# Twelve gate tiles of a two-layer encoder kernel in pairs: seven block products for eight, with the sums of frames on VectorE

## The reference, cut to what matters

```
proj = jnp.einsum('btd,de->bte', x, w_in)          # 512 + 2048 columns
cq = rms_norm(proj[..., :Q_LORA], q_norm_g)        # 4 tiles of 128: query latent
gate = proj[..., Q_LORA:]                          # 16 tiles of 128: one a head
kv = jnp.einsum('btd,de->bte', x, w_dkv)           # key/value latent, 256 + 64
...
out = jnp.einsum('bte,ed->btd', o * jax.nn.silu(gate), w_out_b)
```

## Time and profile before

| | |
|---|---|
| median of 3 runs | 1863.83 us (1863.42 to 1863.83) |
| profiled execution | 1863.33 us, its span 1861.5 us |
| granted TensorE clock, mean | 0.998 |
| VectorE, ScalarE, GpSimd busy | 56%, 40%, 23% of the span |
| HBM | 95 GB/s over the span |

### The profile page before, as it was taken

The page is one execution under the profiler, slowest core; times in us unless marked ns, Lnnn a source line. Parts: engine busy times, 40 slices in busy tenths (PEclk is TensorE's granted clock), DMA queues, the critical chain, the costliest instruction groups (busy, mean ns, idle before and its releaser), DMA issues.

```text
span 1861.5 us, 30229 instructions
## 1 busy us (share of the span) xinstructions
PE 1849.0 (99%) x11250; PEld 1734.6 (93%) x11250; DVE 1046.2 (56%) x1852; ACT 741.8 (40%) x1307; POOL 429.6 (23%) x341
## 2 busy tenths in 40 slices
PE   9999999999999999999999999999999999999998
PEld 8899999999988999999999999999999999998886
DVE  3126565556768512432466676666766679853642
ACT  4234324333422221221355565555555567651100
POOL 0013133223311010000042432434324344400000
PEclk9999999999999999999999999999999999999999
DMA  8120222222255312233302111111121185553521
GB/s 264 57 87 33 76 83 84 72 83 73 70 195 164 131 46 73 83 100 120 100 27 67 42 55 55 56 51 46 51 75 38 30 255 185 189 203 127 166 86 45
DMA packets 162059, 178.91 MB, mean 96 GB/s; under 512 B 23376, under 2 KB 137424, under 8 KB 161712
## 3 DMA queue, kind: packets, MB, share of 16 engines
q1 hardware_dynamic: 155632, 158.08, 26.8%
q10 hardware_dynamic: 6160, 19.14, 2.9%
q0 software_dynamic: 176, 0.43, 0.1%
HBM read 130.86 MB, written 46.76 MB: 95 GB/s over the span
## 4 chain that ended last, share of the span: by engine, by line
PE 94%; DVE 2%; ACT 2%; issue 1%; DMA 1%; POOL 0%; DVEq 0%; ACTq 0%; SPq 0%; POOLq 0%
PE ps L124 27%; PE ps L126 26%; PE ps L125 26%; PE ps L2126 3%; PE ps L2105 2%; PE ps L2104 2%; PE ps L550 1%; PE ps L510 1%; PE ps L576 1%; PE ps L559 1%; PE ps L579 1%; ACT h_p L2239 1%; PE ps L539 1%; PE ps L561 1%; PE ps L2682 1%
## 5 line engine op out<-in xcount | busy, mean ns | idle before, releaser
L2016 POOL TENSOR_SCALAR h_p<-h_p,h_rsum 128x128 f32<-128x128 f32 (+3 forms) x127 | 217.8, 1717 | 420.5 <-DVE h_rsum L2368 420.1
L124 PE MATMUL ps<-act_h,a_w_l 128*128 128x384 f32 x576 | 202.0, 351 | 0.0
L126 PE MATMUL ps<-act_h,a_w_h 128*128 128x384 f32 x576 | 192.9, 335 | 0.0
L125 PE MATMUL ps<-act_l,a_w_h 128*128 128x384 f32 x576 | 192.8, 335 | 0.0
L124 PE MATMUL ps<-act_h,m_c_l 128*128 128x384 f32 x480 | 160.9, 335 | 0.0
L126 PE MATMUL ps<-act_h,m_c_h 128*128 128x384 f32 x480 | 160.4, 334 | 0.0
L125 PE MATMUL ps<-act_l,m_c_h 128*128 128x384 f32 x480 | 160.4, 334 | 0.0
L118 DVE TENSOR_TENSOR h_pt_l<-ps,h_pt_h 128x128 fp32r<-128x128 f32 (+2 forms) x192 | 100.5, 552 | 60.2 <-ACT h_pt_h L113 59.8
L113 ACT ACTIVATE h_pt_h<-ps 128x128 fp32r<-128x128 f32 (+2 forms) x192 | 86.8, 489 | 88.3 <-PE ps L2126 88.1
L2239 ACT ACTIVATE h_p<-ps,h_mx 128x128 f32<-128x128 f32 (+7 forms) x128 | 94.8, 741 | 67.1 <-DVE h_mx L2364 66.7
L124 PE MATMUL ps<-o_w,o_g 128*128 128x512 f32 x288 | 112.3, 390 | 0.0
(11 more groups left out here) (326 smaller groups left out, 4955.0 us busy)
## 6 DMA issues: line engine op xcount, KB each, us to landing
a_w_raw<-in_w_in_a SPq DMA_DIRECT2D x24, 512.0 KB, 5.0
m_c_raw<-in_w_in_b SPq DMA_DIRECT2D x20, 512.0 KB, 4.2
scratch_gate<-m_sg SPq DMA_DIRECT2D x16, 576.0 KB, 5.2
o_w_raw<-in_w_out_b SPq DMA_DIRECT2D x16, 512.0 KB, 5.8
h_gate<-scratch_gate SPq DMA_DIRECT2D x60, 128.0 KB, 2.0
scratch_og<-h_gate SPq DMA_DIRECT2D x60, 128.0 KB, 1.7
s_ct_raw<-in_cache_ckv_turned SPq DMA_DIRECT2D x7, 1024.0 KB, 5.2
o_g_raw<-scratch_og SPq DMA_DIRECT2D x24, 256.0 KB, 4.5
```

Source lines behind the costliest of these rows:

```text
L124: nc.tensor.matmul(out, ll, rh, start=first, stop=False)
L125: nc.tensor.matmul(out, lh, rl, start=False, stop=False)
L126: return nc.tensor.matmul(out, lh, rh, start=False, stop=last)
L2016: nc.gpsimd.tensor_scalar(x, x, rsum[:, u % PB], None, ALU.mult).then_inc(S["p_ready"], 1)
```

## The change

Four gates stay as they were ("direct": 0, 1, 14, 15), and so do the four latent tiles, which move behind the gates. Gates 2 to 13 are taken in six pairs (a, b). For the first two groups of frames, E (early) and M (middle), and the lower and upper half of the 1024 rows (l, u), a pair is a product of 2 x 2 blocks, which is made with seven block products for eight:

- sums of weights (GpSimd, `weight_sums`, 128x512 each): s0 = b_l + b_u, s1 = s0 - a_l, s2 = a_l - b_l, s3 = a_u - s1
- sums of frames (VectorE, 128x1536 each, once for all pairs): t0 = M_l - E_l, t1 = M_u - t0, t2 = t1 - E_l (that is, M_u - M_l), t3 = E_u - t1. The high and the low parts are added one after the other, nine operations in all.
- products: a_l E_l, a_u E_u, s1 t1, s2 t2, s0 t0, s3 M_u, b_u t3; each is 4 row blocks x 3 = 12 matmuls. The third group of frames is multiplied as before, 24 matmuls for each of a and b.

All sums are split in high and low parts like other operands. A product is taken out of PSUM at once and added to what was kept (seven additions of 128x384 on VectorE for a pair, one copy on ScalarE, `first_kept`, `second_kept`, `third_kept`); sigmoids are taken in thirds, from the added result; four of the six gate products of a pair go to GpSimd, since their operands lie in SBUF. A pair has four banks, 0 to 3 or 4 to 7 in turn.

The constants that count semaphores are left out of the diff, and so are the buffers. Loads come two tiles at a time (`load_paired`). The table of the keys' angles is loaded later, and the keys, the norm of the query latent and the splits for the heads stand behind the pairs, in the stretch of the last six direct tiles, whose three thirds are mixed with them:

```diff
+PAIRED = (HEADS - 4) // 2
+DIRECT = [NCQ, NCQ + 1] + list(range(NCQ)) + [NCQ + HEADS - 2, NCQ + HEADS - 1]
+DIRECT_SLOT = [0, 1, 2, 0, 1, 0, 1, 0]
+DIRECT_BANK = [0, 3, 0, 3, 0, 3, 0, 0]
...
+        def load_paired(p):
+            if p == 1:
+                sp.wait_ge(c_done, 2)
+            elif p >= 2:
+                sp.wait_ge(c_done, product_count(p - 2, PRODUCTS))
+            for f in range(2):
+                c = NCQ + 2 + 2 * p + f
+                sp.dma_start(c_raw[pair_set(p)][:, f], w_cols[:, :, c * P:(c + 1) * P]).then_inc(c_loaded[pair_set(p)], 16)
...
+        sp.wait_ge(c_done, column_count(2))
+        sp.dma_start(kvw_raw[:], ...).then_inc(kv_loaded, 16)
+        heads.load_first(sp)
+        sp.wait_ge(c_done, column_count(3))
+        load_direct(5)
+        store_kv(0)
+        store_kv(1)
+        sp.wait_ge(c_done, column_count(4))
+        load_direct(6)
...
     @block.gpsimd
+            s = [sums_of(p, i)[2][:] for i in range(4)]
+            nc.gpsimd.tensor_tensor(s[0], b[:, lower], b[:, upper], ALU.add).then_inc(pooled, 1)
+            nc.gpsimd.tensor_tensor(s[2], a[:, lower], b[:, lower], ALU.subtract).then_inc(pooled, 1)
...
+        weight_sums(0)
+        for p in range(PAIRED):
+            if p + 1 < PAIRED:
+                weight_sums(p + 1)
+            for n, src, f, tg in ((2, first_kept, 0, 0), (3, first_kept, 1, 1), (5, second_kept, 0, 1), (6, third_kept, 1, 0)):
+                pool.wait_ge(sig_done, sigmoid_count(p, n))
+                nc.gpsimd.tensor_tensor(gate_part(p, f, tg), gate_part(p, f, tg), src[:], ALU.mult).then_inc(pooled, 1)
...
     @block.tensor
+        def paired_tiles(p):
+            pe.wait_ge(low_done, SPLIT["pair", p, 1])
+            pair_free(pe, p)
+            if p == 0:
+                pe.wait_ge(gate_out, 1)
+            plain(p, 0, 0, 0, 0, True, True).then_inc(c_done, 1)
+            if p == 0:
+                pe.wait_ge(gate_out, 2)
+            plain(p, 3, 0, 0, 2, True, False)
+            plain(p, 3, 0, 1, 2, False, True).then_inc(c_done, 1)
+            pe.wait_ge(low_done, SPLIT["sums", p, 1])
+            pe.wait_ge(low_done, SPLIT["frames", 1])
+            summed(p, 1, 1, turned_frames(1)).then_inc(c_done, 1)
+            plain(p, 2, 0, 1, 0, True, True).then_inc(c_done, 1)
+            pe.wait_ge(copied, p + 1)
+            pe.wait_ge(low_done, SPLIT["sums", p, 2])
+            pe.wait_ge(low_done, SPLIT["frames", 2])
+            summed(p, 0, 2, turned_frames(2)).then_inc(c_done, 1)
+            pe.wait_ge(combined, combined_count(p, 1))
...
+            summed(p, 1, 0, turned_frames(0)).then_inc(c_done, 1)
...
+        first_of(4)
+        latent(0)
+        columns(4, 1)
+        latent(1)
+        turn_latent(0)
+        columns(4, 2)
+        latent(2)
+        turn_latent(1)
+        first_of(5)
+        latent(3)
...
+        first_of(7)
+        latent(8)
+        turn_latent(7)
+        columns(7, 1)
+        turn_latent(8)
+        columns(7, 2)
...
     @block.scalar
+        def paired_tiles(p):
+            act.wait_ge(c_done, product_count(p, 1))
+            if p:
+                act.wait_ge(pooled, POOLED["gated", p - 1, 1])
+            nc.scalar.copy(first_kept[:], paired_bank(p, 0)).then_inc(copied, 1)
...
+        gate_columns(0)
+        high_pair(0, 0)
+        high_pair(0, 1)
+        high_frames(1)
+        high_sums(0, 0)
+        high_sums(0, 1)
+        gate_columns(1)
+        high_frames(2)
+        high_sums(0, 2)
+        high_frames(0)
+        high_sums(0, 3)
+        high_frames(3)
+        for p in range(PAIRED):
+            paired_tiles(p)
...
+        latent_columns(4)
+        high_columns(6)
+        latent_square(2)
+        turned_high(1)
...
     @block.vector
+        def first_frames():
+            (h0, l0), (h1, l1) = parts(lower, early), parts(lower, middle_cols)
+            nc.vector.tensor_tensor(t_raw[0][:], h1, h0, ALU.subtract).then_inc(combined, 1)
+            nc.vector.tensor_tensor(t_part[0][:], l1, l0, ALU.subtract).then_inc(combined, 1)
+            dve.wait_ge(combined, 2)
+            nc.vector.tensor_tensor(t_raw[0][:], t_raw[0][:], t_part[0][:], ALU.add).then_inc(combined, 1)
...
+        first_frames()
+        second_frames()
+        low_pair(0, 0)
+        low_pair(0, 1)
+        gate_columns(0)
+        low_frames(1)
+        low_sums(0, 0)
+        low_sums(0, 1)
+        gate_columns(1)
+        third_frames()
+        low_frames(2)
+        low_sums(0, 2)
+        low_frames(0)
+        low_sums(0, 3)
+        fourth_frames()
+        low_frames(3)
+        for p in range(PAIRED):
+            paired_tiles(p)
...
+        turned_low_latent(0)
+        low_columns(6)
+        latent(2)
+        turned_low_latent(1)
...
     def bank_free(pe, b):
         if b < 3:
-            pe.wait_ge(gate_out, HEADS - 1)
+            pe.wait_ge(gate_out, gated_count(PAIRED, 2))
         elif b < 6:
-            pe.wait_ge(gate_out, HEADS)
+            pe.wait_ge(spread_out, 3)
```

More of the change, by code:

```diff
@@ L1332, in store_kv @@
             sp.dma_start(kr, krn[:, t % 2, 0]).then_inc(kv_stored[t % 2], 16)
[L1334 to L1351, removed]
@@ L1457, in _, with frames, plain @@
         columns(1, 2)
[L1459 to L1463, removed]
+        def frames(kt, tg):
+            cols = slice(tg * TG, (tg + 1) * TG)
+            return k.act_h[:, kt, cols], k.act_l[:, kt, cols]
+        def plain(p, b, f, half_k, tg, start, stop):
+            s = pair_set(p)
+            for kt in range(nh):
+                at = half_k * nh + kt
+                mm = product(nc, paired_bank(p, b), (c_h[s][:, f, at], c_l[s][:, f, at]), frames(at, tg), start and kt == 0, stop and kt == nh - 1)
+            return mm
@@ new lines, in _ @@
+        first_of(2)
+        columns(2, 1)
+        columns(2, 2)
+        first_of(3)
+        columns(3, 1)
+        columns(3, 2)
+        first_of(4)
[8 more added lines that the diff above has]
+        latent(3)
+        turn_latent(2)
+        columns(5, 1)
+        columns(5, 2)
+        latent(4)
+        turn_latent(3)
+        first_of(6)
+        pe.wait_ge(const_set, 3)
@@ new lines, in _ @@
+        pe.wait_ge(copied, latent_count(NCQ - 1))
+        pe.wait_ge(pooled, POOLED["squares", NCQ - 1])
+        for t in range(NT):
+            mm = nc.tensor.matmul(bank[:, 3, t:t + 1], sums[:, t * P:(t + 1) * P], ones[:], start=True, stop=True)
+        mm.then_inc(ss_done, 1)
+        latent(5)
+        turn_latent(4)
+        columns(6, 1)
+        pe.wait_ge(rep_ready, 1)
+        spread_rows(range(4), 4)
+        spread_rows(range(4, 8), 5)
+        spread_rows(range(8, 9), 3)
+        latent(6)
@@ L1516, in _ @@
+        turn_latent(5)
+        columns(6, 2)
+        latent(7)
+        turn_latent(6)
+        first_of(7)
[4 more added lines that the diff above has]
+        columns(7, 2)
     @block.scalar
@@ new lines, in _ @@
+        latent_square(4)
+        turned_high(3)
+        latent_square(5)
+        turned_high(4)
+        spread_copy(0, range(4), 4)
+        spread_copy(1, range(4, 8), 5)
+        spread_copy(2, range(8, 9), 3)
+        latent_square(6)
+        turned_high(5)
+        high_latent(0)
+        gate_columns(6)
+        high_latent(1)
+        latent_square(7)
+        turned_high(6)
+        high_latent(2)
+        high_latent(3)
+        latent_square(8)
+        turned_high(7)
+        for i in range(WPARTS):
+            heads.split_high(act, i)
@@ new lines, in _ @@
+        second_frames()
[13 more added lines that the diff above has]
+        low_frames(3)
+        for p in range(PAIRED):
+            paired_tiles(p)
+        low_columns(3)
+        low_columns(4)
+        dve.wait_ge(kvh_ready, 1)
@@ new lines, in _ @@
+        round_low(nc, kvw_l[:], kvw_raw[:], kvw_h[:]).then_inc(kvl_ready, 1)
+        low_columns(5)
+        latent(0)
+        latent(1)
+        turned_low_latent(0)
+        low_columns(6)
+        latent(2)
+        turned_low_latent(1)
+        latent(3)
+        turned_low_latent(2)
+        low_columns(7)
+        latent(4)
+        turned_low_latent(3)
+        dve.wait_ge(ss_done, 1)
+        nc.vector.tensor_scalar(ms9[:], bank[:, 3, 0:NT], 1.0 / QL, EPS, ALU.mult, ALU.add).then_inc(ms9_ready, 1)
@@ new lines, in _ @@
+        dve.wait_ge(rs9_ready, 1)
+        nc.vector.tensor_copy(sums[:].rearrange("p (a b) -> p a b", a=NT), rs9[:].rearrange("p (a o) -> p a o", o=1).broadcast_to([P, NT, P])).then_inc(rep_ready, 1)
+        latent(5)
+        turned_low_latent(4)
+        scale_latent(0)
+        scale_latent(1)
+        latent(6)
+        turned_low_latent(5)
+        scale_latent(2)
+        scale_latent(3)
+        low_latent(0)
+        gate_columns(6)
+        low_latent(1)
+        latent(7)
+        turned_low_latent(6)
@@ L1759, in bank_free @@
+        low_latent(2)
+        low_latent(3)
+        latent(8)
+        turned_low_latent(7)
+        for i in range(WPARTS):
```

(8 more changed lines are left out.)

524 lines of the change are left out of this document (369 added, 155 removed).

## The result

The changed kernel takes 1866.78 us (median of 20 runs, 1865.73 to 1867.73), the kernel before 1863.24 (20 runs, 1862.88 to 1863.86): 1.0019 times as long, 95% interval 1.0013 to 1.0026. It is slower by 3.5 us, 0.19%. The interval lies clear of 1.0 but on both sides of the 0.2% that the prediction took as the border; forecast were 4.4 us and 1868.2. The profiled execution took 1866.69 us, 1864.9 of it span (before 1861.5).

What follows compares the result with a forecast made beforehand. TensorE was taken to bound the kernel, matmuls over 99% of the span; -12.5 + 13.4 + 2.0 + 0.75 + 0.75 = +4.4 us gave 1867.7, or 1868.2 on the median's scale; range 1860.5 to 1873.

Steps and rivals of the forecast that it cites:

- Saved, -12.5: Six tile pairs on TensorE: 12 matmuls fewer each, 72 in all, at 0.1733 us, saving 12.5 us.
- the rival of slower matmuls: Pairs' products read other arrays in groups of 12; at 1% more per matmul, 1.4 us lost; 3%.
- First pair, +13.4: TensorE's product 5 waits for ScalarE's copy out of bank 0, from 664.2 to 677.6: 13.4 us lost.
- The meetings, 5.8: First pair: VectorE's frame sums and GpSimd's eight weight sums exclude each other, delaying VectorE's chain by 5.8 us.
- The first rival (1862.4): VectorE and GpSimd hardly meet in the first pair, 5.8 us less, so not slower: 1862.4; 15%.
- Waits on the way (covered): First pair: TensorE's shorter waits for the two gates' banks are covered by product 5's wait and add nothing.
- The clock, +2.0: After the first pair's 9.7 us idle, TensorE restarts at 1.2 GHz: 2.0 us lost, bounds 0 and 2.4.
- The second rival (1866.2): The clock stays up or comes back at once after the first pair's stall: 1866.2, no difference; 20%.
- Product 6, 0.3: First pair: product 6 waits 0.3 us for its sum on VectorE, unless product 5 is slower.
- The tail, +0.75: Latent columns and keys: column 6's late load and its split delay latent tile 3; 0.75 us with the restart.
- The rival of late loads: Loads late in the tail beside gate stores, costing 1.7 us more at latent tile 3: 1871; 10%.
- The end, +0.75: Second head product R1 waits for bank 0, now held by the last gate tile; 0.75 us with the restart.

Runs made afterwards that it cites:

- The run with later sums: Changed kernel with GpSimd making the second pair's four weight sums only when all frame sums are done; 1864.17 us.
- the run with the wait filled: Changed kernel with 44 throwaway matmuls of 384 columns put ahead of the first pair's product 5; 1865.5 us.
- the bank run: Changed kernel with its last gate tile in banks 3 to 5 in place of 0 to 2; 1866.07 us in one run.
- copy first: Changed kernel with only ScalarE's first-pair copy out of bank 0 moved, ahead of the high parts of frame sums three, one and four; 1867.38 us.

## Why the prediction was right

The wait, its releaser and the lower clock behind it came as forecast. Of the 1.0 between the forecast 4.4 and the 3.4 by which the spans differ, the first pair makes -1.0, the tail -0.55 and the end -0.1, the clock +0.2 and what isn't placed +0.45; that the total comes out no further off is in part these signs. The larger chance (0.50) stood on a time over the border of 0.2%; the median lies at 0.19%.

- **Saved, -12.5.** Right: 72 matmuls fewer, and the pairs' matmuls at 0.173 with the clock up; the rival of slower matmuls is out.
- **First pair, +13.4.** Mechanism right, 12.4 in size: product 5 at 676.62 against 664.2. The 1.0 is mostly the chain's plain length: the copy ends at 676.56, of which 5.7 are meetings, so 670.9 without them where I added up 671.6. Most of that is the 0.5 that I added for VectorE's handovers: its last frame sum ends at 674.68, without the meetings 669.0, and the plain sum was 669.3. The rest is a handover to TensorE of 0.06 where I took 0.2, and 0.1 less of meetings.
- **The meetings, 5.8.** Measured 2.9 on the first four sums (11.7 from 639.42 to 651.15, for 8.8) and 2.76 on the other four, 5.7. I had split it 3.3 and 2.5: the first meeting cost VectorE 0.84, not 1.17, and nothing of the second group fell into its wait for ScalarE, since ScalarE's high part then came later by as much. The row that I had taken the price from was misread: there each instruction ended 0.54 (443.59 to 443.05), 1.14 and 1.07 behind the other's end, which is 0.14 to 0.15 short of its full length and not "one full length"; so a meeting costs a little less than I counted. The run with later sums confirms the second group alone. The first rival (1862.4) is out. No run took the first four away by themselves.
- **Waits on the way (covered).** Right: 0.99 and 1.72 for the gates' banks were inside the 12.4, of which 9.12 was idle in one piece (forecast 9.7).
- **The clock, +2.0.** Measured 2.2: products 5 and 6, 24 matmuls, took 6.32 for 4.16. In the run with the wait filled they took 4.57 with the clock up, so 1.7 of it is the clock's, and 0.4 remains there too, at the start of product 5 and at product 6. The lower level held for 4.4 us behind the restart. The row I had scaled from doesn't bear the term out: through the 5.49 us of the program's start the trace of the kernel before has the granted clock at 1.00, as here from 3 to 4 us (third column from the right):

```profile
3.00:4.00 1.00, 1.00 (x6) 1.00 (x6) 0.00 (x0) 0.00 (x0) 0.00 (x0) 1.00 1.07 393
```

So that a lower clock slowed those 28 matmuls isn't shown, and that 2.0 came so near is luck; that the clock would be down at the restart was right. The second rival (1866.2) came nearest in time, but by another road: the clock did fall. The Trainium skill ("TensorE: Matmul & The Clock Gate", Part 1) has the low level as the one that activity lifts; the restart at 676.62 and the rise at 681 agree.
- **Product 6, 0.3.** Hidden by the slow product 5, as forecast.
- **Pairs two to six, nothing.** Right, no wait there.
- **The tail, +0.75.** Mis-sized: 0.2. The list of waits doesn't name it, but the rows do. VectorE's rounding of tile 1, for which TensorE's latent tile 3 waits, and that tile's first matmul:

```profile
858.46 0.28 DVE L118 TENSOR_TENSOR kr_l<-ps,kr_h 128x128 fp32r<-128x128 f32 x1
```

```profile
858.07 0.33 PE L124 MATMUL ps<-act_h,m_c_l 128*128 128x384 f32 x1
...
858.80 0.41 PE L124 MATMUL ps<-m_kvw_h,act_l 128*128 128x320 f32 x1
```

Three matmuls from 858.07 make 858.59; the tile starts at 858.80, when the rounding has ended (858.74). From the load's release at 850.75 that is 8.0 us, where I added up 8.6: ScalarE's split came 3.95 behind the release, not 4.3, and the small instructions behind VectorE's low part took 1.8, not 2.0. The rival of late loads is out.
- **The end, +0.75.** 0.54 of wait and some 0.1 of restart; the bank run shows the cause.
- **Not placed.** -12.5 + 12.4 + 2.2 + 0.2 + 0.65 = 2.95; the spans differ by 3.4. About half of the rest has accrued by the last sigmoid of the stage, 2.54 later than in the earlier trace rows, where the first four terms make 2.3:

```profile
918.91 1.14 ACT L1859 ACTIVATE m_sg<-ps 128x1152 f32<-128x1152 f32 x1 [3.69 <-PE ps L126]
```

No row shows a wait for it, and I leave it open.

What the prediction did not see is how cheap the stall was to remove. It took the chain's length as the price of the change; the runs show that three instructions of VectorE and two of ScalarE, moved, were worth 8.8 us, and that this stretch's work fits beside TensorE with 1.9 us of waits left in the first pair.

## What to carry to other kernels

When TensorE waits on an engine that is itself behind, list what the waiting instruction really needs and see what stands ahead of it in *each* program that feeds it: moving the copy alone moved the wait by one product and gained nothing, moving copy and additions gained 8.8 us. Two engines that exclude each other can be given different inputs (a product with one input in PSUM kept its 0.55 us) or different times, but a delay only pays where the delayed work has slack. Count a long stall of TensorE at more than its length, since what follows it may run at the lower clock: 24 matmuls took 6.32 us here for 4.57.

## What had not been expected of the hardware

A stall of 2.84 us at the second pair's start brought the clock down after it had ended: 1.00 up to the restart at 681.26, 0.50 from 682 to 685, 1.7 us lost. Stalls of 1.72 in the changed kernel and of 1.55 in its variants left it at 1.00; those of 6.36 (later sums) and 7.57 (copy first) saw it fall inside the stall, as the 9.12 did. Beyond its length, each of the four from 2.84 up cost 1.7 to 2.6 us in the matmuls behind it; between 1.72 and 2.84 there is none on record.
